# A depthwise convolution as TensorE matmuls: 128x128 diagonal weights, or 64x64 quadrants placed with tile_position

## What is computed

```python
CONV_K = 31
def conv_branch(h, w_in, dw_w, dw_b, ln_g, ln_b, w_out):
    a, b, z = jnp.split(h @ w_in, 3, axis=-1)
    u = a * jax.nn.sigmoid(b)
    u = lax.conv_general_dilated(
        u, dw_w[:, None, :], window_strides=(1,),
        padding=[(CONV_K // 2, CONV_K // 2)],
        dimension_numbers=('NWC', 'WIO', 'NWC'),
        feature_group_count=CONV_WIDTH) + dw_b
    u = layer_norm(u, ln_g, ln_b)
    u = jax.nn.silu(u) * jax.nn.silu(z)
    return u @ w_out
```

## Time and profile before

| | us |
|---|---|
| runs shown, without a profile | 3393.09 and 3501.49, median 3447.29 |
| the profiled execution | 3373.72 |
| its span on the slowest core (core 3) | 3372.4 |
| spans of the eight cores | 3358.1 to 3372.4 |
| granted TensorE clock of the cores, share of full speed | 0.926 to 0.931 |
| TensorE matmul busy | 2683.0 (80% of the span) |
| DVE, ACT, POOL busy | 1576.3, 1459.7, 871.2 |

### The profile page before, as it was taken

One profiled execution on the slowest core, in us unless ns is written; L12 is line 12 of the kernel. 1 busy time (PEld: TensorE's weight loads), 2 busy tenths in 40 slices (PEclk: granted clock), 3 DMA queues, 4 the chain that ended last, 5 costly groups with the idle time before them and its releaser, 6 DMA issues.

```text
span 3372.4 us, 84232 instructions; the slowest of 8 cores (3358.1 to 3372.4 us)
## 1 busy us (share of the span) xinstructions
PE 2683.0 (80%) x26000; PEld 1549.6 (46%) x26000; DVE 1576.3 (47%) x2413; ACT 1459.7 (43%) x2927; POOL 871.2 (26%) x1293
## 2 busy tenths in 40 slices
PE   0599977886888888887759998688788888888775
PEld 0244433664555555544424443265455555554442
DVE  0410145344666666662341113533466666666336
ACT  0421142342555555553452124324355555555344
POOL 1122100521333333323412210042133333332340
PEclk9999989888999999997769999998899999999876
DMA  9223311665111111114412120133411111111443
GB/s 196 32 40 45 45 20 24 91 97 81 23 28 26 26 26 26 20 27 74 78 14 26 20 32 0 20 39 45 68 26 26 26 26 26 26 20 27 73 76 110
DMA packets 156072, 147.36 MB, mean 44 GB/s; under 512 B 14192, under 2 KB 148464, under 8 KB 155632
## 3 DMA queue, kind: packets, MB, share of 16 engines
q0 software_dynamic: 129680, 108.83, 22.7%
q1 hardware_dynamic: 25952, 33.14, 3.4%
HBM read 226.91 MB, written 17.30 MB: 72 GB/s over the span
## 4 chain that ended last, share of the span: by engine, by line
PE 62%; DVE 13%; ACT 10%; issue 9%; DMA 4%; SPq 1%; POOL 1%; ACTq 0%; DVEq 0%; POOLq 0%
PE PS L425 14%; PE PS L356 11%; PE PS L661 6%; PE PS L406 6%; PE PS L375 6%; PE PS L617 5%; PE PS L574 4%; PE PS L687 3%; DVE ST L642 3%; DVE PT L672 2%; ACT P L646 2%; ACT T L482 2%; PE PS L623 2%; PE PS L628 2%; PE PS L324 2%
## 5 line engine op out<-in xcount | busy, mean ns | idle before, releaser
L646 ACT ACTIVATE P<-PS,ST 128x1024 bf16<-128x1024 f32 (+1 forms) x544 | 523.9, 963 | 352.7 <-DVE ST L642 162.9
L642 DVE TENSOR_REDUCE ST<-PS 128x1 f32<-128x1024 f32 (+1 forms) x544 | 558.1, 1033 | 185.6 <-PE PS L661 121.0
L425 PE MATMUL PS<-U,DG 128*128 128x512 bf16 (+2 forms) x2976 | 474.5, 321 | 34.7 <-DVE U L412 32.8
L652 POOL TENSOR_TENSOR ST<-ST,NEG 128x1 f32<-128x1 f32 x544 | 298.2, 548 | 775.6 <-ACT P L646 773.8
L356 PE MATMUL PS<-HT,WB 128*128 128x512 bf16 (+1 forms) x2048 | 385.6, 348 | 64.4 <-ACT T L475 51.5
L661 PE MATMUL PS<-DD,P 128*128 128x128 bf16 x3584 | 328.7, 224 | 119.3 <-ACT PT L669 82.2
L425 PEld LDWEIGHTS PS<-U,DG 128*128 128x128 bf16 x2976 | 273.2, 99 | 234.6 <-issue 38.2
L661 PEld LDWEIGHTS PS<-DD,P 128*128 128x128 bf16 x3584 | 208.5, 98 | 317.1 <-issue 309.7
L617 PE MATMUL PS<-KT,QT 64*64 64x512 bf16 (+1 forms) x1088 | 214.2, 386 | 151.5 <-ACT P L646 149.1
L669 ACT ACTIVATE PT<-PS 128x512 bf16<-128x512 f32 (+1 forms) x544 | 294.0, 540 | 50.0 <-PE PS L661 46.1
L356 PEld LDWEIGHTS PS<-HT,WB 128*128 128x128 bf16 x2048 | 180.6, 99 | 267.5 <-issue 101.7
(11 more groups left out here) (84 smaller groups left out, 3259.8 us busy)
## 6 DMA issues: line engine op xcount, KB each, us to landing
WB<-nwp POOLq DMA_DIRECT2D x32, 1024.0 KB, 10.2
WB<-ada_w POOLq DMA_DIRECT2D x24, 1024.0 KB, 10.4
WB<-cab POOLq DMA_DIRECT2D x32, 512.0 KB, 6.1
WB<-cz POOLq DMA_DIRECT2D x8, 1024.0 KB, 9.2
WB<-conv_w_out POOLq DMA_DIRECT2D x8, 1024.0 KB, 9.4
WB<-na_w_out POOLq DMA_DIRECT2D x8, 1024.0 KB, 9.5
XS<-xsT SPq DMA_DIRECT2D x1, 6656.0 KB, 26.5
ysT<-T SPq DMA_DIRECT2D x24, 256.0 KB, 2.1
```

What stands on the lines that cost most here:

```text
L425: S.op("pe", lambda e, k=k: e.matmul(ps[:, :nt], lhsT=DG[ub][:, k, :], rhs=U[ub][:, uo + k - 15:uo + k - 15 + nt], start=(k == 0), stop=(k ...
L642: S.op("dve", lambda e: e.reduce_max(out=stt[:, 0:1], in_=sp_[:, 0:nk], axis=AX.X, negate=True), R=rsk, W=[stk])
L646: S.op("act", lambda e: e.activation(out=P_[:, 0:nk], in_=sp_[:, 0:nk], func=AF.Exp, bias=stt[:, 0:1], scale=1.0, accum_out=stt[:, 2:3]), ...
L652: S.op("pool", lambda e: e.tensor_tensor(out=stt[:, 3:4], in0=stt[:, 2:3], in1=NEG1[:], op=ALU.pow), R=[smk, "NEG1"], W=[("RS", ui % 2)])
```

## The change

The 64x64 quadrants of the array are addressed one by one. Two buffers of 31 weights of 64 columns take DG's place: DGA holds on each partition the tap weights of its own channel, DGB those of the channel 64 partitions away (table DWWR). ID64 is a 64-wide identity on both partition halves. U1 is a copy of U with the two partition halves exchanged, made by two DMAs on SP's queue. Taps 0 to 15 go straight (quadrants (0, 0) and (64, 64), data U, weights DGA), taps 16 to 30 crossed (quadrants (64, 0) and (0, 64), data U1, weights DGB). Quadrants on rows 0 to 63 add up in the first bank of PS2, those on rows 64 to 127 in the second, for every tile; ACT then takes the first bank with the bias to a temporary in SBUF, and DVE adds the second bank to it into GT. U1, DGA and DGB have one buffer each; the building of weights and the copy for block n+1 (`prep`) are written behind conv(n). During the convolution `statps` has only the second bank of PS3. The tap tables are bf16 and load on POOL's queue.

```diff
-        DWW = sb("DWW", [128, 2, NCH, CK], F32)
+        DWW = sb("DWW", [128, 2, NCH, CK], BF16)
+        DWWR = sb("DWWR", [128, 2, NCH, CK], BF16)
+        ID64 = sb("ID64", [128, 64], BF16)
...
+        SP_ALL = [(2, 0), (2, 1)]
+        state["spool"] = SP_ALL
+
         def statps():
-            k = state["sp"] % 2
+            pool_ = state["spool"]
+            t, h = pool_[state["sp"] % len(pool_)]
             state["sp"] += 1
-            return PS[2][:, k * 512:k * 512 + 512], ("PS", 2, k)
+            return PS[t][:, h * 512:h * 512 + 512], ("PS", t, h)
...
-        S.dma("sp", dq["aux"], DWW[:], dww_d, W=["DWW"])
+        S.dma("pool", dq["idb"], DWW[:], dww_d, W=["DWW"])
+        S.dma("pool", dq["idb"], DWWR[:], dwwr_d, W=["DWWR"])
...
+        S.op("dve", lambda e: e.tensor_tensor(out=ID64[:], in0=IDB[:, 0:64], in1=IDB[:, 64:128], op=ALU.add), R=["IDB"], W=["ID64"])
...
-            DG = [sb("DG%d_%d_%d" % (i, g.gi, k), [128, CK, 128], BF16, lst) for k in range(2)]
+            U1 = sb("U1_%d_%d" % (i, g.gi), [128, UL], BF16, lst)
+            DGA = sb("DGA%d_%d" % (i, g.gi), [128, CK, 64], BF16, lst)
+            DGB = sb("DGB%d_%d" % (i, g.gi), [128, CK, 64], BF16, lst)
+            NS0 = (CK + 1) // 2
...
+
+            def prep(n):
+                ub = n % 2
                 S.op("pool", lambda e: e.tensor_tensor(
-                    out=DG[ub][:], in0=IDB[:].unsqueeze(1).to_broadcast([128, CK, 128]),
-                    in1=DWW[:, j, n, :].unsqueeze(2).to_broadcast([128, CK, 128]), op=ALU.mult),
-                    R=["IDB", "DWW"], W=[("DG", ub)])
+                    out=DGA[:], in0=ID64[:].unsqueeze(1).to_broadcast([128, CK, 64]),
+                    in1=DWW[:, j, n, :].unsqueeze(2).to_broadcast([128, CK, 64]), op=ALU.mult),
+                    R=["ID64", "DWW"], W=["DGA"])
+                S.op("pool", lambda e: e.tensor_tensor(
+                    out=DGB[:], in0=ID64[:].unsqueeze(1).to_broadcast([128, CK, 64]),
+                    in1=DWWR[:, j, n, :].unsqueeze(2).to_broadcast([128, CK, 64]), op=ALU.mult),
+                    R=["ID64", "DWWR"], W=["DGB"])
+                S.dma("sp", dq["u1"], U1[0:64, :], U[ub][64:128, :], R=[("U", ub)], W=["U1"])
+                S.dma("sp", dq["u1"], U1[64:128, :], U[ub][0:64, :], R=[("U", ub)], W=["U1"])
 
             def conv(n):
                 ub = n % 2
                 for ti, (t0, nt) in enumerate(g.tiles):
-                    ps, pk = projps()
+                    banks = [(PS[2][:, 0:512], ("PS", 2, 0)), (PS[2][:, 512:1024], ("PS", 2, 1))]
                     uo = g.uoff(t0)
-                    for k in range(CK):
-                        S.op("pe", lambda e, k=k: e.matmul(ps[:, :nt], lhsT=DG[ub][:, k, :], rhs=U[ub][:, uo + k - 15:uo + k - 15 + nt],
-                                                            start=(k == 0), stop=(k == CK - 1)),
-                             R=[("DG", ub), ("U", ub)], W=[pk])
-                    S.op("act", lambda e: e.activation(out=GT[:, n, t0:t0 + nt], in_=ps[:, :nt], func=AF.Identity,
+                    for sl in range(NS0):
+                        for (ih, jh) in ((0, 0), (1, 1), (1, 0), (0, 1)):
+                            own = (ih == jh)
+                            k = sl if own else NS0 + sl
+                            if k >= CK:
+                                continue
+                            first = (sl == 0)
+                            last = (k == NS0 - 1) if own else (k == CK - 1)
+                            src, skey = (U[ub], ("U", ub)) if own else (U1, "U1")
+                            dg, dkey = (DGA, "DGA") if own else (DGB, "DGB")
+                            bk, bkey = banks[ih]
+                            S.op("pe", lambda e, ih=ih, jh=jh, k=k, src=src, dg=dg, bk=bk, first=first, last=last: e.matmul(
+                                bk[64 * jh:64 * jh + 64, :nt], lhsT=dg[64 * ih:64 * ih + 64, k, :],
+                                rhs=src[64 * ih:64 * ih + 64, uo + k - 15:uo + k - 15 + nt],
+                                start=first, stop=last, tile_position=((64 * ih, 64 * jh) if (ih or jh) else None)),
+                                R=[dkey, skey], W=[bkey])
+                    t1, k1 = tmp()
+                    S.op("act", lambda e: e.activation(out=t1[:, :nt], in_=banks[0][0][:, :nt], func=AF.Identity,
                                                        bias=PV[:, 5 + j, n:n + 1], scale=1.0),
-                         R=[pk, "PVEC"], W=[("GT", n, ti)])
+                         R=[banks[0][1], "PVEC"], W=[k1])
+                    S.op("dve", lambda e: e.tensor_tensor(out=GT[:, n, t0:t0 + nt], in0=banks[1][0][:, :nt], in1=t1[:, :nt], op=ALU.add),
+                         R=[banks[1][1], k1], W=[("GT", n, ti)])
...
+            state["spool"] = [(3, 1)]
             glu(0)
+            prep(0)
             for n in range(NCH):
                 if n + 1 < NCH:
                     glu(n + 1)
                 conv(n)
+                if n + 1 < NCH:
+                    prep(n + 1)
                 ada_step()
...
+            state["spool"] = SP_ALL
```

More of the change, by code:

```diff
@@ L161, in build_program @@
     dww_d = din("dww", [128, 2, NCH, CK])
+    dwwr_d = din("dwwr", [128, 2, NCH, CK])
     ckT_d = din("ckT", [2, D, PAST])
@@ L213, in build_program @@
         PS = [st.enter_context(nc.psum_tensor("PS%d" % k, [128, 1024], F32)) for k in range(4)]
-        dq = {k: S.new_dma_sem("dq_" + k) for k in ("ld", "w0", "w1", "w2", "aux", "idb", "v1", "kc0", "kc1", "vc0", "vc1", "tm0", "tm1", "ko0", "ko1")}
+        dq = {k: S.new_dma_sem("dq_" + k) for k in ("ld", "w0", "w1", "w2", "aux", "idb", "v1", "u1", "kc0", "kc1", "vc0", "vc1", "tm0", "tm1", "ko0", "ko1")}
         wsem = [dq["w0"], dq["w1"], dq["w2"]]
@@ L845, in make_in_maps @@
          for j in range(2) for n in range(8)], axis=0))
-    shared = dict(pv=pv, adab=adab, dww=dww, tm=tm, ident=ident, ada_w=a["ada_w"], cab=cab, cz=cz,
+    dwwr = np.ascontiguousarray(np.roll(dww, -64, axis=0))
+    shared = dict(pv=pv, adab=adab, dww=dww, dwwr=dwwr, tm=tm, ident=ident, ada_w=a["ada_w"], cab=cab, cz=cz,
                   conv_w_out=a["conv_w_out"], nwp=nwp, na_w_out=a["na_w_out"])
```

## The result

The change makes the kernel slightly slower. Its median is 3407.97 us over 12 runs (3399.45 to 3630.36) beside 3375.52 us over 11 runs of the kernel before (3370.53 to 3668.95). The ratio is 1.009, 95% interval 1.007 to 1.011. Executions in which some cores ran longer at a lower granted clock are left out of the ratios, and such cores out of the means that are said to be over six cores. I had forecast 3336 us, about 1.7% faster.

The account below looks back on a forecast made before the run. TensorE was taken to bound both groups, S and P. The terms -85 + 17 - 7 + 5 + 12 = -58 us gave 3316 us on the profiled execution, forecast as 3336 us, range 3265 to 3450.

Parts of the forecast that it names:

- A slot streams four quadrants at once, 0.218 us: Convolution on TensorE: up to four 64x64 matmuls of 512 columns overlap, 0.218 us a slot, 16 slots a tile.
- The rival in which column halves take turns: Convolution: column halves do not overlap, a slot takes 0.436 us, about +145 us, 3540 us in all; chance 0.12.
- the loads pace nothing: Against the rival that weight loads pace the short tiles: P's slots at twice 0.123, about +50, 3386 us; chance 0.06.
- The wait per tile, 1.83 us: Tile ends in S: TensorE waits for ACT's, then DVE's evacuation of PS2, 1.83 us, three times per block.
- The clock, +12 us: TensorE's granted clock falls slightly in the bursts with pauses: +6 us in S and +6 in P.
- P, -7 us: Prompt group's convolution layers together: longer plain cycles and late weights against shorter blocks elsewhere, -7 us, clock apart.
- The late conditioning weights: P, layer 0: next conditioning weights, issued behind POOL's building, land 5 us after the next block's end; +6 us.
- The relief of 5 us in the blocks that had waited for a DVE reciprocal: P: four blocks whose convolution waited for a PSUM bank start at once, finishing about 5 us earlier; -20 us.
- The U1 copy at nothing: The swapped copy of U on SP's queue lands after 2.6 us, under POOL's building, and costs nothing.
- Bare building ahead of each last block, 14 + 3: S, ahead of each layer's last block: no GLU covers POOL's building, +14 us, and +3 us for the clock.
- POOL quicker with two bf16 inputs: Rival: POOL builds DGA and DGB in half the time, some -35 us more, 3301 us; chance 0.22.
- LayerNorm +5: LayerNorm's first sums wait for the last evacuation of PS2, about 1.2 us, four times: +5 us.

Follow-up runs that it names:

- the bank pairs: The changed kernel with odd convolution tiles in PS1's two banks and even tiles in PS2's: ratio 0.9763 to the kernel before.
- background first in S alone: The changed kernel with background steps (sums of squares, DVE scaling, ACT) written ahead of conv(n) in S only: ratio 0.9993 to the kernel before.
- the background first: The changed kernel with the background steps written ahead of conv(n) instead of behind it, in S and P: ratio 1.0011 to the kernel before.
- all three: The changed kernel with background steps ahead of conv(n), two buffers each for DGA, DGB and U1, and tiles in two bank pairs: ratio 0.9493 to before.

## Why the prediction was wrong

- *A slot streams four quadrants at once, 0.218 us*: right, to the digit, and by that a block of S at 17.5 us (forecast 17.3). The rival in which column halves take turns is out, and the loads pace nothing in S: a slot of 512 columns shows no longer distance than the full array did.
- *The wait per tile, 1.83 us*: right in kind, in its two parts and nearly in size (1.99 us between tiles in the rows above, 2.0 to 2.2 by the bank pairs).
- *What is in the queues of ACT and DVE beside that*: here the prediction failed. It gave DVE an add per tile and asked only who waits for the add. It did not ask what the add is now ahead of. The scaling had run beside conv(n), and went behind it, onto POOL's building and ahead of the GLU's evacuation. I had listed POOL's building as "under the GLU, vanishes" by TensorE's time alone, and had not asked which other engine's work lay in that stretch. That is 41 us in S (background first in S alone), against a forecast of -62 with the clock's share and a measured -15.
- *The clock, +12 us*: mis-sized with it. Behind the 3.8 us wait the GLU has 1.2 GHz. In S, layer 0, part of the dip stays with the background first (0.92 to 0.94 over the six cores) and goes only when the tile waits go too: 0.96 to 0.98, and GLUs of 11.4 us, in all three. P was granted 0.79 and 0.75 where it had had 0.89.
- *P, -7 us*: measured +40, with the clock's share forecast at +6. The late conditioning weights were foreseen and are there (8.9 us waited for). Not foreseen was what stands ahead of a tile's evacuation on ACT. DVE, ACT and PE in P, layer 0 (core 5):

```profile
616.56 3.35 DVE L339 RECIPROCAL TR<-TR 128x512 f32<-128x512 f32 x1 [7.36 <-ACT TR L337]
```

```profile
620.86 1.39 ACT L352 ACTIVATE HT<-T,MODS 128x512 bf16<-128x512 f32 x2 [4.40 <-DVE T L349]
...
624.10 0.48 ACT L462 ACTIVATE T<-PS,PVEC 128x256 f32<-128x256 f32 x1
```

```profile
624.73 0.27 PE L456 MATMUL PS<-U,DGA 64*64 64x256 bf16 x1 [3.05 <-ACT T L462]
```

  ACT's L352 waits for DVE's reciprocal and the scaling behind it, and the tile's evacuation (L462) stands behind L352 and the GLU's sigmoids, with a table load of 1.28 us ahead of them. It is the chain that held a PSUM bank in the kernel before; the change took its wait from the bank and brought back part of it at the tile's end. The three longest waits at tile ends, 3.05, 3.04 and 3.78 us, are behind it. The waits at tile ends of that stage come to 15.3 + 3.2 = 18.5 us, where 8 x 1.35 = 11 were forecast. Plain blocks take 16 to 17 us in the mean, against 12.6 and, with late weights, 14.1. The relief of 5 us in the blocks that had waited for a DVE reciprocal came to about 4: from one conditioning step to the next 21.3 us (607.55 to 628.82) beside 25.1 before (616.95 to 642.06).
- *The U1 copy at nothing*: wrong in P. It was priced by a median landing of 2.6 us from attention, which says nothing of layer 0 with its loads, and as one landing, where it is two in a row. It is worth 20 us there once POOL's building is out of its way, and 9 in each S; in the changed kernel the two overlap, and in P, layer 0, 6.5 us show as its own. P was to change by -1 us with the clock's share and rose by 40; how these 41 us divide among its waits and the clock no run shows.
- *Bare building ahead of each last block, 14 + 3*: the 14 is right. TensorE waits 6.6 us (3.8 + 2.8) and 7.7 (4.8 + 2.9) for it on core 5, against 6.5 and 7.3.
- *POOL quicker with two bf16 inputs*: no, 3.50 us for half the elements of 6.83.
- *LayerNorm +5*: measured +3.

The page "SBUF — State Buffer" of the Trainium skill (Who interferes with whom) has the rule that I should have weighed: a DVE operation with two SBUF inputs and a GpSimd operation that reads SBUF exclude each other for a whole instruction, and the one that comes second waits. This case's trace agrees: 0.48 us become 3.5 us, as long as POOL's instruction, and a DVE operation with one input in PSUM is not touched (L412 took its 0.69 us at 1892.36, in the middle of POOL's building). The trace of the kernel before had it already (durations in ns, min/median/max; the longest beside POOL's 6.8 us):

```profile
L340 DVE SCALAR_TENSOR_TENSOR T<-XP,AMOD,TR x64: 474/476/7792, 191.5 to 3112.2; 128x256 f32<-128x256 f32 x64
```

## What to carry to other kernels

When an edit gives an engine new work, look at what that engine had been running ahead of its place in the program while it had nothing there. It will be held back, and it has to be laid against everything that starts when the new work ends, other engines included. If a matmul train gets shorter, double the PSUM banks behind it first: here that one edit was worth 110 us. A transfer that was hidden by a long stage is to be priced in the busiest stage it will run in, not by its median, and once for each transfer that has to wait for another.

## What was not expected of the hardware

- Four 64x64 matmuls on the four quadrants, with different moving data and weights, cost one stream of 512 columns (0.218 us a slot), with all loads hidden. The rows of before showed pairs alone.
- A DVE scaling of 0.48 us takes 3.5 us beside a POOL tensor_tensor of 3.5 us, and 7 us beside one of 6.8 us, while the POOL instruction is slowed by little (3.49 and 3.67 us, 3.50 for both without DVE's work). DVE's own tensor_tensor of 1984 bf16 elements takes 2.22 us, less than POOL's 3.5.
- A transfer of 70 KB from SBUF to SBUF, 2.0 us to landing at the median, took 8.1 us while weights were being loaded; two of them in a row held TensorE for 9.9 us.
